# Attention in a two-block transformer kernel: weights of the softmax scaled before they are turned, values padded with zeros as the stationary operand

## The reference, cut to what matters

```python
h = rms_norm(x, g)                                # 256 x 1024
q, k, v, gate, u = split(h @ w_in)                # each 256 x 512
q, k = partial_rope(q), partial_rope(k)           # per head of 64
s = einsum("bhqd,bhkd->bhqk", q, k) * 64 ** -0.5
s = where(kpos <= qpos, s, -1e30)
p = softmax(s)
attn = einsum("bhqk,bhkd->bhqd", p, v)            # 256 x 512
rec = gelu(gate) * rg_lru(conv(u))                # 256 x 512
out = concatenate([attn, rec], -1) @ w_out        # 256 x 1024
x = x + rms_norm(out, g_post)
```

## Time and profile before

| | |
|---|---|
| median of 3 runs | 1665.07 us (lowest 1664.26, highest 7304.23) |
| profiled execution | 1664.19 us, span 1662.4 us |
| PE busy | 1651.9 us (99%) |
| PE weight loads | 1419.0 us (85%) |
| DVE busy | 1218.8 us (73%) |
| ACT busy | 920.2 us (55%) |
| POOL busy | 148.9 us (9%) |
| chain that ended last | PE 94%, DVE 3% |
| granted clock of PE (PEclk) | 9, the top digit, in all 40 slices |
| moved by DMA | 358.47 MB, mean 216 GB/s |

### The profile page before, as it was taken

The page is one execution under the profiler, slowest core; times in us unless marked ns, Lnnn a source line. Parts: engine busy times, 40 slices in busy tenths (PEclk is TensorE's granted clock), DMA queues, the critical chain, the costliest instruction groups (busy, mean ns, idle before and its releaser), DMA issues.

```text
span 1662.4 us, 22774 instructions
## 1 busy us (share of the span) xinstructions
PE 1651.9 (99%) x8740; PEld 1419.0 (85%) x8740; DVE 1218.8 (73%) x1632; ACT 920.2 (55%) x1396; POOL 148.9 (9%) x210
## 2 busy tenths in 40 slices
PE   9999999999999999999999999999999999999998
PEld 7888888888888888888899888888888889988887
DVE  6888776788889777776788776655766668986564
ACT  6655577645555455545566455545544458655453
POOL 1100100000211001020010010100002011310000
PEclk9999999999999999999999999999999999999999
DMA  8987553787859876787555457554667546357561
GB/s 296 333 264 261 168 192 103 243 292 260 284 178 326 268 247 221 249 304 257 194 170 189 160 177 262 195 191 144 222 215 247 191 142 203 110 177 241 189 194 66
DMA packets 99356, 358.47 MB, mean 216 GB/s; under 512 B 11184, under 2 KB 11696, under 8 KB 99248
## 3 DMA queue, kind: packets, MB, share of 16 engines
q1 hardware_dynamic: 92736, 334.73, 59.8%
q0 software_dynamic: 6368, 22.21, 4.2%
q10 hardware_dynamic: 144, 0.07, 0.0%
HBM read 355.85 MB, written 1.12 MB: 215 GB/s over the span
## 4 chain that ended last, share of the span: by engine, by line
PE 94%; DVE 3%; DMA 1%; ACT 1%; issue 1%; SPq 0%; DVEq 0%; POOLq 0%; POOL 0%; ACTq 0%
PE dn L549 29%; PE gu L503 21%; PE tp L533 11%; PE gu L533 11%; PE gu L538 6%; PE tp L538 6%; PE dn L518 3%; PE tp L466 1%; PE dn L533 1%; DVE w_lo L1790 1%; DMA raw<-in_weights 1%; PE dn L503 1%; PE dn L538 0%; PE tp L645 0%; DMA x<-in_x_in 0%
## 5 line engine op out<-in xcount | busy, mean ns | idle before, releaser
L1790 DVE TENSOR_TENSOR w_lo<-raw,w_hi 128x1024 fp32r<-128x1024 f32 x518 | 635.0, 1237 | 301.6 <-ACT w_hi L1151 297.1
L1151 ACT ACTIVATE w_hi<-raw 128x1024 fp32r<-128x1024 f32 x520 | 547.5, 1056 | 461.6 <-PE dn L549 140.4
L503 PE MATMUL gu<-w_hi,hT 128*128 128x512 f32 x1056 | 328.8, 392 | 1.7 <-DVE w_lo L1783 1.2
L549 PE MATMUL dn<-w_hi,actT_hi 128*128 128x512 f32 x608 | 239.2, 393 | 0.0
L549 PE MATMUL dn<-w_hi,actT_lo 128*128 128x512 f32 x608 | 237.4, 390 | 0.0
L549 PE MATMUL dn<-w_lo,actT_hi 128*128 128x512 f32 x608 | 236.9, 390 | 0.0
L503 PEld LDWEIGHTS gu<-w_hi,hT 128*128 128x128 f32 x1056 | 195.5, 188 | 42.8 <-DVE hT L1798 1.7
L503 PE MATMUL gu<-w_lo,hT 128*128 128x512 f32 x528 | 205.8, 390 | 0.0
L533 PE MATMUL gu<-hT,w_hi 128*128 128x512 f32 x832 | 199.1, 391 | 0.3 <-DVE hT L1798 0.3
L533 PE MATMUL tp<-hT,w_hi 128*128 128x512 f32 x832 | 199.0, 391 | 0.0
L533 PEld LDWEIGHTS gu<-hT,w_hi 128*128 128x128 f32 x832 | 155.1, 188 | 33.0 <-DVE hT L1798 1.0
(11 more groups left out here) (354 smaller groups left out, 1844.0 us busy)
## 6 DMA issues: line engine op xcount, KB each, us to landing
raw<-in_weights SPq DMA_DIRECT2D x561, 512.0 KB, 4.4
arena<-in_ada_w SPq DMA_DIRECT2D x72, 512.0 KB, 4.4
post_row<-in_post_rows POOLq DMA_DIRECT2D x10, 512.0 KB, 5.6
pre_row<-in_pre_rows POOLq DMA_DIRECT2D x10, 512.0 KB, 7.0
mod_row<-mod POOLq DMA_DIRECT2D x9, 512.0 KB, 9.9
shift_row<-mod POOLq DMA_DIRECT2D x5, 512.0 KB, 8.7
x<-in_x_in SPq DMA_DIRECT2D x4, 256.0 KB, 6.2
arena<-in_c_rows POOLq DMA_DIRECT2D x2, 512.0 KB, 9.1
```

The lines of the kernel that those rows point to most:

```text
L503: m = pe.matmul(bank, h[:, k, t * P:(t + 1) * P], w[:, r, kk * 512:(kk + 1) * 512], start=k == 0 and q == 0, stop=k == KT - 1 and q == 2)
L549: m = pe.matmul(dn[:, t, c], a[:, k, :], w[:, r, c], start=start and q == 0, stop=stop and q == 2)
L1151: act.activation(o, i, ACT.Copy, **kw).then_inc(done, 1)
L1790: dve.tensor_tensor(w_lo[:, r, :], raw[:, n % RAW, :], w_hi[:, r, :].bitcast(F32), ALU.subtract).then_inc(lo_ready, 1)
```

## The change

The scaling by one over the sum is moved ahead of the turning: for each head, DVE's new `normed(h)` takes the reciprocal of the two sums and multiplies the exponentials in place, and `exp_turned(h)` waits for it (`exp_normed`) where it waited for `exp_ready`. The values are copied by ACT into `xn` (free by then, it held queries and keys) as 128 columns a head, of which 64 are zeros on alternating sides; DVE writes the zeros with a memset. `weighted(h)` has these 128 columns stationary and the turned exponentials moving, and two heads add up in one region of 128 partitions (their features) by 256 tokens. The result therefore needs no turning: `attn_turned` and DVE's `weighted` are gone, and ACT and DVE take upper and lower parts from `dn`, two of the four feature tiles at a time, as soon as four heads are done. What the output projection waits for changes with it.

```diff
@@ -216,11 +216,11 @@
         igate = part(4108, LT, TOK)
         th = part(5132, LT, TOK)
         decay = part(6156, LT, TOK)
-        vtok = part(7180, TT, HEADS * HD)
         masked = [part(at, 3 * P) for at in (10252, 10636, 12556, 12940)]
         expo = [part(11020, 3 * P), part(11404, 3 * P)] + [v[:, :, :].rearrange("p a b -> p (a b)")[:, 0:3 * P] for v in (silu, act_tok)]
         expT = [part(at, 3 * P) for at in (2060, 2444, 11788, 12172, 0, 384, 11788, 12172)]
-        attn = part(12556, TT, HEADS * HD)
+        v_pad = xn[:, :, :]
+        v_quarters = xn[:, :, :].rearrange("p t (q a d) -> p t q a d", a=4, d=HD)
         qk = xn[:, :, :].rearrange("p t (h d) -> p t h d", h=2 * HEADS)
         rope_t = silu[:, :, :].rearrange("p a b -> p (a b)")
         rope_u = act_tok[:, :, :].rearrange("p a b -> p (a b)")
@@ -296,7 +296,8 @@
         lru_tanh, lru_decay, lru_ratio, lru_root, rec_ready = sem("lru_tanh"), sem("lru_decay"), sem("lru_ratio"), sem("lru_root"), sem("rec_ready")
         roped, qkT_psum, qkT_hi, qkT_lo = sem("roped"), sem("qkT_psum"), sem("qkT_hi"), sem("qkT_lo")
         scores_done, masked_ready, exp_ready = sem("scores_done"), sem("masked_ready"), sem("exp_ready")
-        expT_psum, expT_ready, attn_psum, attn_ready = sem("expT_psum"), sem("expT_ready"), sem("attn_psum"), sem("attn_ready")
+        v_padded = sem("v_padded")
+        expT_psum, expT_ready, attn_psum, exp_normed = sem("expT_psum"), sem("expT_ready"), sem("attn_psum"), sem("exp_normed")
 
         sc_gate, sc_mixed, half_read = sem("sc_gate"), sem("sc_mixed"), sem("half_read")
         sc_low, sc_summed = sem("sc_low"), sem("sc_summed")
@@ -556,12 +557,10 @@
             def tokens_of(a_hi, a_lo, tiles):
                 return {t: (a_hi[:, :, t * P:(t + 1) * P], a_lo[:, :, t * P:(t + 1) * P]) for t in tiles}
 
-            def out_proj(s, n, order, parts, first=True, between=lambda i: None, apart=()):
+            def out_proj(s, n, order, parts, first=True, apart=()):
 
                 for t in range(TT):
                     for i, k in enumerate(order):
-                        if t == 0:
-                            between(i)
                         pe.wait_ge(mix_lo, parts[k][t])
                         if t and i == len(order) - 2:
                             transposed(s + 1, 0)
@@ -791,7 +790,7 @@
                     m.then_inc(gates_done, 1)
 
                 def exp_turned(h):
-                    pe.wait_ge(exp_ready, h + 1)
+                    pe.wait_ge(exp_normed, h + 1)
                     if h == 3:
                         pe.wait_ge(qkT_lo, HEADS // 2)
                     elif h:
@@ -805,20 +804,16 @@
                     pe.wait_ge(expT_ready, h + 1)
                     if h == 0:
                         pe.wait_ge(ab_evac, 8)
-                    eT, v = expT[h], slice(h * HD, (h + 1) * HD)
-                    pe.matmul(dn[:, 1, v], eT[:, 0:P], vtok[:, 0, v], start=True, stop=True)
-                    pe.matmul(dn[:, 1, 512 + h * HD:512 + (h + 1) * HD], eT[:, P:2 * P], vtok[:, 0, v],
-                              start=True, stop=False)
-                    m = pe.matmul(dn[:, 1, 512 + h * HD:512 + (h + 1) * HD], eT[:, 2 * P:3 * P], vtok[:, 1, v],
-                                  start=False, stop=True)
-                    if h == HEADS - 1:
-                        m.then_inc(attn_psum, 1)
-
-                def attn_turned(t):
-                    pe.wait_ge(attn_ready, t + 1)
-                    for k in range(4):
-                        m = pe.transpose(tp[:, t, k * P:(k + 1) * P], attn[:, t, k * P:(k + 1) * P], ident[:])
-                    m.then_inc(mixT_psum, 1)
+                        pe.wait_ge(v_padded, 1)
+                    eT, v, o = expT[h], slice(h * P, (h + 1) * P), dn[:, 1, h // 2 * TOK:(h // 2 + 1) * TOK]
+                    if h % 2 == 0:
+                        pe.matmul(o, v_pad[:, 0, v], eT[:, 0:TOK], start=True, stop=False)
+                        pe.matmul(o[:, P:TOK], v_pad[:, 1, v], eT[:, TOK:TOK + P], start=False, stop=False)
+                    else:
+                        pe.matmul(o[:, P:TOK], v_pad[:, 1, v], eT[:, TOK:TOK + P], start=False, stop=False)
+                        m = pe.matmul(o, v_pad[:, 0, v], eT[:, 0:TOK], start=False, stop=True)
+                        if h % 4 == 3:
+                            m.then_inc(attn_psum, 1)
 
                 opening(s, n0, lambda t: None, lambda group: pe.wait_ge(ab_evac, group + 1))
                 lru_slot(0, 0, 0)
@@ -865,8 +860,7 @@
                 weighted(6)
                 weighted(7)
                 pe.wait_ge(ab_evac, 10)
-                out_proj(s, n0 + 20, [4, 5, 6, 7, 0, 1, 2, 3], [[3, 4]] * 4 + [[1, 1]] * 2 + [[2, 2]] * 2,
-                         between=lambda i: attn_turned(i - 3) if i in (3, 4) else None, apart=(4, 5))
+                out_proj(s, n0 + 20, [4, 5, 6, 7, 0, 1, 2, 3], [[3, 3]] * 2 + [[4, 4]] * 2 + [[1, 1]] * 2 + [[2, 2]] * 2, apart=(4, 5))
 
             def sc(s, n0):
                 def bank_freed(q):
@@ -1432,9 +1426,9 @@
                     act.wait_ge(slot_used, n0 + 18 + 2 * pair)
                     act.activation(gelu[:, pair_of(pair), :], lru_bank(pair), ACT.Gelu_apprx_tanh).then_inc(ab_evac, 1)
 
-                def attn_upper(t):
-                    act.wait_ge(mixT_psum, t + 1)
-                    copy(hT_hi[:, 0:4, t * P:(t + 1) * P], tp[:, t, :].rearrange("p (k c) -> p k c", k=4), mix_hi)
+                def attn_upper(b):
+                    act.wait_ge(attn_psum, b + 1)
+                    copy(hT_hi[:, 2 * b:2 * b + 2, :], dn_bank(2 + b).rearrange("p (k c) -> p k c", k=2), mix_hi)
 
                 opening(s, n0, taken, lambda t: None)
                 act.wait_ge(ada_used, ADA_0)
@@ -1466,7 +1460,7 @@
                 after_slots(n0 + 13, 1)
                 act.wait_ge(slot_used, n0 + 16)
                 for t in range(TT):
-                    copy(vtok[:, t, :], dn[:, 1, t * 512:(t + 1) * 512], ab_evac)
+                    copy(v_quarters[:, t, :, 0:4:3, :], dn_bank(2 + t).rearrange("p (q e d) -> p q e d", e=2, d=HD), ab_evac)
                 exponential(4)
                 exponential(5)
                 exp_taken(3)
@@ -1651,7 +1645,7 @@
                     m.then_inc(y_ready, 1)
 
                 def y_upper(b):
-                    act.wait_ge(mixT_psum, 2 + b + 1)
+                    act.wait_ge(mixT_psum, b + 1)
                     for i in (2 * b, 2 * b + 1):
                         m = act.activation(hT_hi[:, 2 + i, :], y_turned_at(i), ACT.Copy, scale=ssd_norm[:, i:i + 1])
                     m.then_inc(mix_hi, 1)
@@ -2137,15 +2131,18 @@
                     dve.wait_ge(ab_evac, 9 + pair)
                     dve.tensor_tensor(gelu[:, pair_of(pair), :], gelu[:, pair_of(pair), :], rgate[:, pair_of(pair), :], ALU.mult).then_inc(rec_ready, 1)
 
-                def weighted(t):
-                    dve.tensor_tensor(attn[:, t, :].rearrange("p (h d) -> p h d", h=HEADS),
-                                      dn[:, 1, t * 512:(t + 1) * 512].rearrange("p (h d) -> p h d", h=HEADS),
-                                      soft[:, 3, :, t].unsqueeze(2).broadcast_to([P, HEADS, HD]), ALU.mult).then_inc(attn_ready, 1)
-
-                def attn_lower(t):
-                    c = (slice(None), slice(0, 4), slice(t * P, (t + 1) * P))
-                    dve.wait_ge(mix_hi, 3 + t)
-                    lower(hT_lo[c], tp[:, t, :].rearrange("p (k c) -> p k c", k=4), hT_hi[c], mix_lo)
+                def normed(h):
+
+                    dve.wait_ge(exp_ready, h + 1)
+                    then(dve.reciprocal(soft[:, 3, h, :], soft[:, 2, h, :]))
+                    e = expo[h % 4]
+                    dve.tensor_scalar(e[:, 0:P], e[:, 0:P], soft[:, 3, h, 0:1], None, ALU.mult)
+                    dve.tensor_scalar(e[:, P:3 * P], e[:, P:3 * P], soft[:, 3, h, 1:2], None, ALU.mult).then_inc(exp_normed, 1)
+
+                def attn_lower(b):
+                    c = (slice(None), slice(2 * b, 2 * b + 2), slice(None))
+                    dve.wait_ge(mix_hi, 3 + b)
+                    lower(hT_lo[c], dn_bank(2 + b).rearrange("p (k c) -> p k c", k=2), hT_hi[c], mix_lo)
 
                 dve.wait_ge(late_consts, ALL_LATE)
                 dve.memset(lx[:, :, 0:LRU_CONV - 1], 0.0)
@@ -2157,6 +2154,8 @@
                 maximum(0)
                 maximum(1)
                 qk_lower(1)
+                normed(0)
+                normed(1)
                 convolved(1)
                 after_slots(n0 + 10, 2)
                 maximum(2)
@@ -2169,28 +2168,30 @@
                 maximum(5)
                 dve.wait_ge(lru_decay, LT)
                 then(dve.tensor_tensor(rgate[:, :, :], decay[:, :, :], decay[:, :, :], ALU.mult))
+                normed(2)
                 qk_lower(3)
+                dve.memset(v_quarters[:, :, :, 1:3, :].rearrange("p t q a d -> p (t q) (a d)"), 0.0).then_inc(v_padded, 1)
+                normed(3)
```

(9 more changed lines are left out.)

## The result

| | before | changed |
|---|---|---|
| median | 1663.99 us (17 runs, lowest 1663.21) | 1667.95 us (17 runs, 1666.60 to 1670.54) |
| ratio, 95% interval | | 1.0023 (1.0017 to 1.0030) |
| profiled execution, span | 1664.19, 1662.4 us | 1667.50, 1665.7 us |
| PE busy / DVE busy | 1651.9 / 1218.8 us | 1652.4 / 1223.1 us |

The change costs 4.0 us, a quarter of a per cent; 1668.3 us was forecast, from pauses and work that add up to 3.6 us. One of the 17 executions of the kernel before took 7304.23 us; it is counted and doesn't move the median.

What follows compares the result with a forecast made beforehand. PE, always at work, was taken to bound the kernel. Pauses of 4.15 us less 0.6 us of work gave +3.6 us, 1667.8 or 1668.7 us by base; forecast 1668.3 us, range 1665.9 to 1671.5.

Steps and rivals of the forecast that it cites:

- What bounds the kernel, and where a delay goes: Whole kernel: PE is always at work, nothing behind the stage absorbs delay, so PE's loss comes out at the end.
- PE's own work: Attention stage and output projection: products +0.45 us, two turnings gone -0.9, a wait of about 0.15 gone; sum -0.6 us.
- The fourth rival: Products with the values: narrow fp32 pass costs as much as the wide one, +1.8 us, 1670.1 us; chance 0.05.
- `normed`: DVE's scaling per head: 0.77 us from first issue until PE may go on, bounds 0.65 and 1.0 us.
- h = 0: Before head 0's turning: scaling stands behind the second pair's lower part on DVE, so PE pauses 1.0 us.
- h = 1, 5 to 7: Before these heads' turnings: no pause; head 1 done a value slot early, the others have 2 to 3 us to spare.
- h = 2: Before head 2's turning: scaling stands behind the square of the decays; pause 2.45 us, 1.7 queue place, 0.8 scaling.
- h = 3: Before head 3's turning: fourth turning of queries and keys, lower part, memset and scaling delay PE 0 to 0.4 us, 0.1 taken.
- h = 4: Before head 4's turning: a weights' lower part and maxima stand ahead on DVE; pause 0.6 us, bounds 0.3 and 1.2.
- The clock: Around head 2: pause then transposes may halve PE's clock, +3 us for one column block, 1671.3 us; chance 0.1.
- Faster, because the pauses don't reach the end: Whole kernel: PE catches up and only the saved turnings remain, 1664.5 us; chance 0.05.
- Weights late in the output projection: Output projection: added scaling pushes weights' lower parts beyond the eight-slot ring, PE waits for weights, 1671 us; chance 0.05.

Runs made afterwards that it cites:

- Padded values alone: Changed kernel without its scaling, the turning waiting for ACT's exponentials as before: 1663.08 us, -1.0 us against the kernel before.
- all early: Changed kernel with the scalings of heads 0, 2, 3, 4 and 5 moved to earlier places in DVE's queue: 1662.98 us, again 1663.04.
- head 2 early: Changed kernel with head 2's scaling moved ahead of the square of the decays in DVE's queue: 1664.79 us, +0.7 over before.
- long pause: Changed kernel with one unused 128x1024 DVE product ahead of head 2's scaling: 1669.56 us, +5.5 over before.
- first set of the changed kernel: The changed kernel's original 17 runs, 1667.95 us; it was later run again unaltered as a second set, 1668.24 us.
- scaling alone: Kernel before with only the scaling moved ahead of the turning; values, products and turnings of the result kept: 1668.60 us, +4.5 over before.
- pause filled: Changed kernel with nine unused 128x512 products on PE before head 2's turning: 1668.75 us, +4.7 over before.
- second trace: Each kernel run again unaltered for another profile: kernel before 1664.64 us, stage 76.38; changed kernel 1668.24 us, stage 79.97.

## Why the prediction was right, point by point

**What bounds the kernel, and where a delay goes.** Borne out: stage and median move together. Padded values alone -1.1 and -1.0 us, all early -1.2 and -1.1, head 2 early +0.4 and +0.7, long pause +5.5 and +5.5. Ten of the thirteen rows agree within 0.4 us; in the first set of the changed kernel, with the scaling alone and with the pause filled the median is 0.8 to 1.2 us more than the one trace explains.

**PE's own work.** "-0.6 us" was -1.1: the output projection took 22.89 us instead of 23.91, -1.02 as forecast for the turnings and the wait. The mis-sized term is the products, +0.45 forecast, about -0.05 measured (the stage with the padded values alone is 1.09 us shorter, its output projection 1.04). The pass of 256 columns takes 0.215 us (0.229 was read from the gates), that of 128 columns 0.11 (0.115), as the rows from 263.81 to 264.46 show for pairs of passes; by these numbers eight heads take about 5.1 us against 5.16 before (5.0 in my reading), where 5.5 was to be a sign. The fourth rival (the narrow pass as dear as the wide) is out.

**`normed`.** Reciprocal 154 ns, multiplications 286 and 347 ns, and 0.70 to 0.75 us from the first issue to the end where 0.77 was forecast (at head 2: 252.12 to 252.87).

**h = 0.** 1.0 us forecast, 0.40 and about 1.2 in two executions. The step was right for the trace it was read from. Its input, 2.81 us from PE's turning to DVE's lower part, is at the upper end of what this distance takes (2.13 to 2.93), and eight of 14 traces have the lower end.

**h = 1, 5 to 7.** No pause, as forecast.

**h = 2.** 2.45 forecast, 2.58 measured; the square began at 250.86 (251.8 was forecast). That is before the 251.5 that was named as a sign of being wrong. It doesn't touch the step: head 0's pause was shorter, and PE asked 0.95 us earlier as well, so the difference of the two, which makes the pause, stayed.

**h = 3.** 0.1 forecast (0 to 0.4), 0.44 measured, just outside. The larger part is 0.24 us ahead of the memset: it began 0.85 us after the lower part before it (254.58 to 255.43), where 0.61 was counted, and 0.16 of that is listed as issue. The memset's own 0.91 us did not count in full, since the next instruction began after 0.83.

**h = 4.** 0.6 forecast, 0.54 measured. The forecast has 0.1 us of head 3 twice (3.45 + 0.1 is already the 3.55), so by its own steps it would be 0.7.

**Sum.** 4.15 us of pauses forecast, 3.96 measured; with the work, +3.6 forecast, +2.9 by the measured terms, +2.75 from one timeline to the other (and 79.97 - 76.38 = +3.6 from second trace to second trace). That the median came within 0.35 us of 1668.3 is in part luck. Against the first trace, head 0 (by 0.6 us) and the products (0.5) were forecast too dear, head 3 (0.3) too cheap. The base was put between 1664.2 and 1665.07, a median of three runs, where 17 runs gave 1663.99. And 0.4 to 1.2 us of the 3.96 are in neither pair of stages. The fall of the clock, which the forecast left out, may account for some of it; how much is open. The lower end of the range, 1665.9, does not follow from its terms: 1664.19 + 2.6 is 1666.8.

**The clock.** This was the step that was wrong. The fall was given a chance of 0.1 and a price of 3 us; it comes in at least half of the executions and costs 1.5 us in the stage, since the level came back after 3.4 us, before the slowed column block had ended, where I had let the whole block run at the lower one. My argument against it ("1.5 us did nothing") compared a pause of 1.5 us with one of 2.45 us plus 0.7 us of transposes. The profile of the changed kernel happened to be one of the executions without it, so the sign "a fall between 251 and 260" did not show there. The Trainium skill ("TensorE: Matmul & The Clock Gate", sections "Why this matters for your kernels" and "Part 4: PE-mode transpose") points at this place: a pause between bursts of products, then transposes that don't count as work. The runs agree on the pause, with a fall in at least 33 of 63 executions at 2.3 to 2.8 us and in 5 of 5 at 3.5 us. Whether the transposes count as work no run here separates; at 3.5 us the clock fell before them.

An estimate from these numbers: half of the executions at 1.5 us are 0.8 us on average, which makes 3.6 to 4.4 us of the stage's 2.75 to 3.6, and 3.96 was measured. That is no proof. The executions at 0.998 are 0.9 us slower than the others in the changed kernel's first set and no slower in its second, and with the pause filled the time did not come down.

**The other rivals.** Faster, because the pauses don't reach the end: out, they do (head 2 early). Weights late in the output projection: out, no wait of PE is listed there.

**What stays open.** What makes a slot land later in some executions, and so sets the distance at head 0; how much of the median is the fall of the clock, and with it why the filled pause was no faster than the changed kernel; and single waits outside the stage that differ between executions (at L534 0.3 us before and 0.97 after, the same instructions), which blur every difference of two traces by some half a microsecond.

## What to carry to other kernels

New work for an engine that has idle time is free only if it is done before the consumer asks, and that depends on what stands ahead of it in the engine's queue. Here the same 0.8 us of scaling made a pause of 2.6 us behind an instruction that waits, and none in front of it. Compare the time at which the consumer asks with the end of the instruction ahead in the queue, step by step down the stage; that gave three of the four pauses here within 0.35 us, and the fourth as well as its input, which differs between executions by 0.8 us. When a pause of the length seen here opens on PE, look at the mean clock of all executions, not at one profile: four of the six traces with such a pause show no fall.

## What the runs showed of the hardware

- The granted clock fell to half behind a listed wait of PE of 2.3 to 2.8 us followed by 0.7 us of transposes, in 33 to 47 of 63 executions, in some executions of a kernel and not in others: for 3.4 us in two traces, not at all in four. In a wait of 3.5 us it fell 2.6 us after PE had stopped and stayed down for 6.8 us in the one trace; all five executions of that kernel read 0.998.
- Half clock made a column block of 2.96 us last 4.4 us, since the level came back before its end.
- A tensor-scalar with a column as its factor took 286 ns for 128x128 and 347 for 128x256, where immediates take 220 and 285.
- A memset of 128x1024 took 912 ns, that of 128x512 485: 0.83 ns a column, less than the 1.2 ns a column of a two-operand instruction.
- An fp32 pass of 128 columns took 0.11 us, about the same as one of 64 columns (0.105); one of 256 columns took 0.215, and 0.229 in the gates. With twice as many columns moved for each head, eight heads took no longer than before.
